# Sixteen-expert diffusion step on one Trainium2 core: earlier third and later expert blocks, expert rows fetched by plain loads, first input weights issued after the fourth modulation block

## The reference, cut to what matters

```
h  = rmsnorm(x) * (1 + scale1) + shift1;  P = h @ w_in          # 12 MB of weights
x  = x + gate1 * concat(A, B, C, D) @ w_out                     # attention, scan, window attention, DFT
h2 = rmsnorm(x) * (1 + scale2) + shift2
x  = x + gate2 * MoE(h2)         # 16 experts, top-1 of 4 groups, then top-2 experts in it
     a = h2 @ w_gate[e]; u = h2 @ w_up[e]; z = silu(a) * u * gates[:, e]; out += z @ w_down[e]
```

## Time and profile before

| | us |
|---|---|
| median of three runs | 1331.93 |
| the profiled execution, its own time | 1326.58 |
| its span, first to last instruction | 1324.6 |
| TensorE busy | 1183.9 |
| VectorE / ScalarE / GpSimd busy | 541.4 / 422.4 / 283.5 |

### The profile page before, as it was taken

One profiled execution on the slowest core, in us unless ns is written; L12 is line 12 of the kernel. 1 busy time (PEld: TensorE's weight loads), 2 busy tenths in 40 slices (PEclk: granted clock), 3 DMA queues, 4 the chain that ended last, 5 costly groups with the idle time before them and its releaser, 6 DMA issues.

```text
span 1324.6 us, 19868 instructions
## 1 busy us (share of the span) xinstructions
PE 1183.9 (89%) x7788; PEld 543.6 (41%) x7788; DVE 541.4 (41%) x1309; ACT 422.4 (32%) x732; POOL 283.5 (21%) x375
## 2 busy tenths in 40 slices
PE   3899899789879999999869989979896999999995
PEld 0555555354423333333234655546343333333332
DVE  1274676733532222221455756585145122211217
ACT  2223444431323333333221334443122433323332
POOL 1230373220021211110510325350102021111022
PEclk9999889789989999999979997997996999999997
DMA  9749531655779999999730313063614999999962
GB/s 365 269 149 161 99 96 69 230 201 223 293 286 390 390 387 382 403 397 377 268 111 2 134 64 97 16 244 134 257 61 166 407 394 385 401 391 379 381 238 92
DMA packets 52722, 324.13 MB, mean 245 GB/s; under 512 B 8457, under 2 KB 8905, under 8 KB 34080
## 3 DMA queue, kind: packets, MB, share of 16 engines
q1 hardware_dynamic: 37568, 286.87, 56.1%
q0 software_dynamic: 13792, 31.42, 9.2%
q10 hardware_dynamic: 1280, 4.72, 0.9%
HBM read 318.70 MB, written 24.31 MB: 259 GB/s over the span
## 4 chain that ended last, share of the span: by engine, by line
PE 68%; DVE 16%; DMA 11%; issue 2%; ACT 2%; another core or an unknown queue 1%; SPq 0%; DVEq 0%; ACTq 0%
PE ps L1917 32%; PE ps L1558 18%; DMA ring<-moe_w_up 7%; PE ps L1806 7%; DVE attT L1155 3%; DVE dbuf L1134 2%; DMA ring<-ada_w 2%; PE ps L1906 2%; PE ps L1569 2%; PE ps L1592 2%; PE ps L1729 1%; PE ps L1700 1%; DVE small L1260 1%; DMA ring<-w_out 1%
## 5 line engine op out<-in xcount | busy, mean ns | idle before, releaser
L1917 PE MATMUL ps<-ring,dbuf 128*32 128x512 f32 x3072 | 433.2, 602 | 18.3 <-ACT dbuf L1003 7.2
L1917 PE MATMUL ps<-extra,dbuf 128*32 128x512 f32 x1536 | 210.7, 595 | 3.6 <-DMA ring<-moe_w_up 3.6
L1917 PEld LDWEIGHTS ps<-ring,dbuf 128*32 128x32 f32 x3072 | 119.3, 111 | 220.6 <-issue 213.4
L1558 PE MATMUL ps<-ring,extra 128*128 128x512 f32 (+1 forms) x384 | 149.4, 549 | 0.0
L1558 PE MATMUL ps<-extra,ring 128*128 128x384 f32 (+1 forms) x384 | 124.1, 470 | 7.6 <-ACT extra L810 5.1
L1917 PEld LDWEIGHTS ps<-extra,dbuf 128*32 128x32 f32 x1536 | 61.2, 110 | 133.3 <-issue 133.1
L744 POOL DMA_INDIRECT expert_rows<-big,lst x28 | 26.5, 946 | 417.6 <-DVE big L1476 417.6
L999 ACT ACTIVATE big<-ps 96x512 f32<-96x512 f32 x32 | 34.5, 1079 | 226.6 <-issue 169.9
L1558 PEld LDWEIGHTS ps<-ring,extra 128*128 128x128 f32 x384 | 73.9, 194 | 69.5 <-issue 66.0
L1454 DVE COPY dbuf<-ps 128x384 f32<-128x384 f32 x32 | 17.8, 558 | 202.6 <-PE ps L1906 199.1
L1558 PEld LDWEIGHTS ps<-extra,ring 128*128 128x128 f32 x384 | 73.9, 202 | 52.9 <-issue 9.4
(11 more groups left out here) (300 smaller groups left out, 1484.2 us busy)
## 6 DMA issues: line engine op xcount, KB each, us to landing
ring<-moe_w_up SPq DMA_DIRECT2D x30, 2048.0 KB
ring<-ada_w SPq DMA_DIRECT2D x24, 2048.0 KB
ring<-moe_w_down SPq DMA_DIRECT2D x18, 2048.0 KB
ring<-moe_w_gate SPq DMA_DIRECT2D x16, 2048.0 KB
extra<-moe_w_gate SPq DMA_DIRECT2D x16, 2048.0 KB, 17.1
extra<-moe_w_down SPq DMA_DIRECT2D x14, 2048.0 KB, 20.0
ring<-w_in SPq DMA_DIRECT2D x12, 2048.0 KB
ring<-w_out SPq DMA_DIRECT2D x4, 2048.0 KB
```

What stands on the lines that cost most here:

```text
L1558: ins = pe.matmul(out, a, b, start=(n == 0), stop=(n == len(pairs) - 1))
L1917: return pe.matmul(p[QT * g:QT * (g + 1), :], a, w, start=start, stop=stop, tile_position=(0, QT * g))
```

## The change

- SP no longer holds block 3. In layer 0 block 4 is held until the first gather has landed, in layer 1 no block is (`HELD`). The look at the overflow number comes after block 5; where there is overflow, blocks 3 to 5 are loaded a second time after it (`blocks_again`).
- The clearing of the table and the six scatters of records are inside POOL's overflow branch.
- The expert rows come back through six plain loads, 512 KB each, issued by SP after a layer's last block and before the next layer's first. All rows are loaded; those of the last two experts are multiplied by zero: `kept` is 0 or 1. ScalarE (ACT) multiplies tile by tile the first choice (three copies of 1024 columns with a scale per row, after the last turn's copy), DVE adds the second choice times its factor, one operation a tile, for tile 2 too.
- `completed` adds both halves of PE's part to y first, then does gate and x with 1024 columns each. POOL does no sums and no clearing of `yr`.
- The first `w_in` block waits until all four `ada` blocks have landed.

```diff
+HELD = [4, None]
...
-                    if l and i_n == 1:
-                        for t in range(NT):
-                            sp.wait_ge(d_yr[t], 32 * l)
+                    if l == 0 and i_n == len(ADA_FIRST):
+                        for b in range(len(ADA_FIRST)):
+                            sp.wait_ge(landed[SLOT_OF[ISSUE[0][b]]], 16)
...
-                        if j == 3:
-                            overflow_weights(l)
+                        if j == HELD[l]:
                             sp.wait_ge(d_g[0], 16 * (NE // 2 * l + 1))
...
+                        expert_block(l, j, landed[n])
+                        if j == ESLOTS - 1:
+                            overflow_weights(l)
...
+                for b in range(2):
+                    sp.wait_ge(d_sc[b], 16 * ((NE - LATE) // 2) * (l + 1))
+                for t in range(NT):
+                    for k in range(2):
+                        sp.dma_start(yr[k][:, t, :], yrow.rearrange("(t p k) d -> t k p d", t=NT, k=2)[t, k]).then_inc(d_yr[t], 16)
...
+                    if last:
+                        act.wait_ge(s_late, l + 1)
+                        for t in range(NT):
+                            act.wait_ge(d_yr[t], 32 * (l + 1))
+                            act.activation(yr[0][:, t, :], yr[0][:, t, :], ACT.Copy, scale=kept[:, t:t + 1]).then_inc(s_kept, 1)
...
-                    step(dve.tensor_tensor(y, y, yr[1][:, t, :], ALU.add))
-                    step(dve.tensor_tensor(y, y, gate[:, min(t, 1), :], ALU.mult))
-                    step(dve.tensor_tensor(x[:, t, :], x[:, t, :], y, ALU.add))
+                    step(dve.scalar_tensor_tensor(out=y, in0=yr[1][:, t, :], scalar=kept[:, NT + t:NT + t + 1], in1=y, op0=ALU.mult, op1=ALU.add))
...
+                        y = yr[0][:, t, b * 512:(b + 1) * 512]
+                        release(dve, dve.tensor_tensor(y, y, p, ALU.add), job)
+                    y = yr[0][:, t, :]
+                    step(dve.tensor_tensor(y, y, gate[:, min(t, 1), :], ALU.mult))
+                    dve.tensor_tensor(x[:, t, :], x[:, t, :], y, ALU.add).then_inc(s_x, 1)
```

More of the change, by code:

```diff
@@ L390, in hybrid_step @@
         d_skew = sem("skew_rows_written")
-        d_tab, d_hrow, d_slot = (sem(n) for n in ("table_cleared", "hidden_rows_stored", "slots_scattered"))
+        d_hrow = sem("hidden_rows_stored")
         s_inpl, s_lst = sem("slot_columns_ready"), sem("slot_lists_ready")
@@ L396, in hybrid_step @@
         s_sel, s_pay, s_ovt, s_nov = (sem(n) for n in ("choices_ready", "slots_ready", "overflow_table_ready", "overflow_count_ready"))
-        s_late, s_sum2, d_init = sem("late_rows_known"), sem("tile_two_summed"), sem("expert_rows_first_written")
+        s_late, s_kept, d_init = sem("late_rows_known"), sem("rows_of_kept_picks"), sem("expert_rows_first_written")
         sync_passed, pool_passed = sem("sync_passed"), sem("pool_passed")
-        ov = [{k: sem(f"ov{l}_{k}") for k in ("weights_landed", "tensor", "vector", "scalar", "list_landed", "gathered", "stored")} for l in range(L)]
+        ov = [{k: sem(f"ov{l}_{k}") for k in ("weights_landed", "tensor", "vector", "scalar", "list_landed", "gathered", "stored",
+                                        "table_cleared", "slots_scattered", "blocks_again")} for l in range(L)]
         table = nc.dram_tensor("slot_table", (NE * T, 4), U32, kind="Internal").ap()
@@ L524, in overflow_weights @@
                     for q in range(3, ESLOTS):
-                        if BEFORE["expert", l, q]:
-                            block_read(sp, BEFORE["expert", l, q])
+                        blk = ("expert", l, q)
+                        sp.wait_ge(landed[SLOT_OF[blk]], 16 * NTH[blk])
                     sp.wait_ge(s_ovt, l + 1)
@@ L535, in overflow_weights, with expert_block @@
                         sp.sem_inc(sync_passed, 1)
+                    for q in range(3, ESLOTS):
+                        expert_block(l, q, o_["blocks_again"])
+            def expert_block(l, j, landed_):
+                kind_, e_ = queued(j)
+                view, kc = {"a": (moe_w_gate, KC), "u": (moe_w_up, KC), "dn1": (moe_w_down, FC)}[kind_]
+                sp.dma_start(slot_of(SLOT_OF["expert", l, j]).rearrange("p (k n) -> p k n", k=kc),
+                             view[l].rearrange("e (p k) n -> e p k n", p=P)[e_]).then_inc(landed_, 16)
             for l in range(L):
-                gview = moe_w_gate[l].rearrange("e (p k) n -> e p k n", p=P)
-                uview = moe_w_up[l].rearrange("e (p k) n -> e p k n", p=P)
-                dview = moe_w_down[l].rearrange("e (p k) n -> e p k n", p=P)
                 for i_n, blk in enumerate(ISSUE[l]):
@@ L570, in _ @@
                                      src.rearrange("(k p) n -> p k n", p=P)).then_inc(landed[n], 16)
+                moved(sp, ("lst", l))
+                sp.wait_ge(s_pay, l + 1)
+                for s in range(2):
+                    for b in range(2):
+                        moved(sp, ("gbc", l, 1, s, b))
+                for b in range(2):
+                    sp.wait_ge(d_sc[b], 16 * ((NE - LATE) // 2) * (l + 1))
+                for t in range(NT):
+                    for k in range(2):
+                        sp.dma_start(yr[k][:, t, :], yrow.rearrange("(t p k) d -> t k p d", t=NT, k=2)[t, k]).then_inc(d_yr[t], 16)
             for t in range(NT):
@@ L703, in _ @@
                 gather(1)
-                pool.wait_ge(s_pay, l + 1)
-                for t in range(NT):
-                    for k in range(2):
-                        pool.indirect_dma_start(table, bass.IndirectOffsetOnAxis(slotu[:, t, k:k + 1], 0), pay[:, t, k, :],
-                                                None).then_inc(d_slot, 16)
                 pool.wait_ge(s_lst, 2 * l + 2)
@@ L713, in _ @@
                 with pool.If(n_ov > 0):
+                    pool.dma_start(table.rearrange("(p r) w -> p (r w)", p=P), slots0[:, 0:4 * NE * NT]).then_inc(o_["table_cleared"], 16)
+                    pool.wait_ge(o_["table_cleared"], 16)
+                    pool.wait_ge(s_pay, l + 1)
+                    for t in range(NT):
+                        for k in range(2):
+                            pool.indirect_dma_start(table, bass.IndirectOffsetOnAxis(slotu[:, t, k:k + 1], 0), pay[:, t, k, :],
+                                                    None).then_inc(o_["slots_scattered"], 16)
+                    pool.wait_ge(o_["slots_scattered"], 16 * 2 * NT)
                     pool.wait_ge(s_ovt, l + 1)
-                    pool.wait_ge(d_slot, 16 * 2 * NT * (l + 1))
                     with pool.Fori(0, n_ov) as r:
@@ L732, in _ @@
                         gather(e + 2)
-                    if e == EXP_PER_BODY:
-                        for s in range(2):
-                            for b in range(2):
-                                moved(pool, ("gbc", l, 1, s, b))
-                        for k in range(2):
-                            step(pool.memset(yr[k], 0.0))
                     if l == 0 and e == 1:
```

40 lines of the change are left out of this document (6 added, 34 removed).

## The result

The changed kernel takes **1312.7 us** (median of four executions, 1309.87 to 1314.31) where the kernel before takes 1329.76 in the same comparison (1322.63 to 1332.45): ratio 0.988, 95% interval 0.983 to 0.992. It is 1.2% faster.

A forecast was written before the change was run, and what follows sets the result against it. The chain was taken as mostly TensorE, with the expert stages' weight stream slightly slower and late near their end. Terms summed to -6.9 us, 1331.93 to 1325.0; half of 3.2 us surplus lead gave 1323.4, range 1316 to 1330.5.

The forecast's parts named there:

- I take the waits as gone: -1.9 and -5.8: Expert stages, layers 0 and 1: earlier blocks 3 to 5 end TensorE's waits for up blocks, -1.9 and -5.8 us.
- counted half of 3.2 us: Sum: lead gained, 10.9 us, exceeds the waits seen, 7.7, by 3.2; half counted for slower executions' longer waits.
- Two blocks and two gathers are 5.0 MB, less than the 5.93 that were moved: Layer 0's expert stage: with block 3 issued early, no backlog is left at 388 us, when block 6 goes out.
- The tails, "-0.3" and "+0.9": End of each layer after the last down product, new DVE order: -0.3 us in layer 0, +0.9 in layer 1.
- They were covered, except that they slowed DVE's: Tails: POOL's three sums, which go, were covered except for slowing DVE's; no size given.
- The start, "+0.4": Start: first input block issued after the last modulation block lands; first input product 0 to 0.9 us later, taken as +0.4.
- my bound of +2: Start: upper bound of the loss, +2 us, if the input block's issue is slower still.
- The head, "-0.2": Head of the expert stages: table clearing and scatters are covered; DVE loses one operation, -0.2 us, layer 1 alone.
- The first: Rival 1, head and tails: the gaps beside POOL's gathers go too, 9.3 us in all, 1314.1 us; chance 0.15.
- The rule that I held against it: Against rival 1: by the instruction-fetch rule the gaps come from the loop that ended before, and stay; time stays 1323.4.
- The second rival: Rival 2, expert stages: the stream stays late, only half of the 7.7 us goes, 1328.9 us; chance 0.20.
- The third: Rival 3, tails: row loads hold up ACT before the last down product, 9 us a layer, 1343 us; chance 0.05.

The follow-up runs named there:

- before_start: The kernel before with only the start's wait added (first input weights wait for the four modulation blocks): 1330.09 us, ratio 1.0027.
- before_dvesum: The kernel before with POOL's three wide additions of tile 2 in the tails done by DVE: 1322.94 us against 1326.47, ratio 0.998.
- nostart: The changed kernel without its start's wait for the four modulation blocks: 1308.25 us (before 1328.33 beside it).
- before_again: The kernel before, unchanged, profiled a second time: 1324.17 us.
- after_again: The changed kernel, unchanged, run once more beside two versions of it: 1312.01 us (before 1327.43).

## Why the prediction was wrong

**The rows of one execution were taken as the kernel's.** That is the root. The profiled execution of before had gaps that ended in "remote" on ACT, DVE and POOL, and they delayed PE by some 16.5 us in all. While PE stood at the head of layer 0, the stream of blocks ran on and won lead, and in the tails POOL's sums got out of DVE's way. So the same rows showed too small a price at two other places: 7.7 us of waiting for blocks, where five executions of before and its variants without gaps have 12.4 to 16.6, and tails 3.1 and 2.5 us too short. The total did not tell them apart, 1326.58 and 1324.17 us, but partly by luck, since the first execution was 7.3 us ahead before its first gap.

**"I take the waits as gone: -1.9 and -5.8", -7.7: too small, this step failed.** The method was right and its two numbers came from the wrong execution: the waits at which I capped the gain, and the backlog of layer 0, which is 7.8 us and not 3.0 where PE does not stand at the head. In the executions without gaps the waits are large enough to use most of the lead of some 15 us: early blocks alone gave -13.2 us, of which 8.3 to 12.5 are seen as less waiting in the stages (12.4 to 16.6 down to 4.1). I had seen the hint (the slower executions "must have lost their 5 us somewhere, and waits of the stream are what can grow") and counted half of 3.2 us for it. That the waits of layer 0 would vanish was also wrong: 2.1 us stayed. "Two blocks and two gathers are 5.0 MB, less than the 5.93 that were moved" used the 17.7 us of the gap; between block 4 (376.78) and block 6 (388.68) there are 11.9 us, in which 343 GB/s are 4.1 MB, so by my arithmetic 0.9 MB or 2.4 us of backlog were left. Block 3 went out at 363.15 and not near 354, since PE must have read its slot first, which I had overlooked; it cost little, as from 372 to 376.78 the link moved only 177 GB/s.

**The tails, "-0.3" and "+0.9": right against the rows, wrong for the kernel.** From the last copy to the last `normalize` it is 21.7 us before and after in layer 0 (652.10 to 673.80 after), and 22.6 and 23.0 in layer 1 (1282.05 to 1305.06). Against executions without gaps the new order gains 3.1 and 2.0, and with SP's loads it gave -5.4. "They were covered, except that they slowed DVE's" was the sentence in which the term was hidden: the slowing is 5.6 us in the tail of layer 0 (2.79 + 3.25 + 3.25 less 3 x 1.23) and 4.5 in layer 1 (1.65 + 3.25 + 3.25), on the path, and I left it without a number.

**The start, "+0.4": wrong.** The first input block is used 13.03 us after its issue, where I had 8.06 and 2 for the small loads. The block of 8.06 us was not alone either: SP issued the next behind it within 2.1 us, and three more by 293.6. What differs is what moved beside the first block: 3.78 MB in 13.03 us at 290 GB/s, 0.93 of them POOL's small loads, against 2.45 MB in 8.06 us at 304 GB/s. Between the two profiled executions the first input product is 3.7 us later; over all of them it begins at 42.7 to 46.2 us without the wait and at 45.8 to 47.7 with it. Measured: +2.7 alone and 3.8 to 4.4 in the changed kernel, beyond my bound of +2. The clock has no part that can be told: the stretch ahead of the first input product had 0.84 with the wait in `before_start` and 0.59 without it in `before_dvesum` (33.5 to 46 us), and the 240 products took 82.8 to 85.8 us without the wait too, 85.77 in `nostart`.

**The head, "-0.2": not settled.** The table's move gave 1.2 alone and 2.6 when undone, and neither is clear of the noise. In layer 1 I had looked only at the gather behind the early blocks. It landed 4.33 us after its issue, but the store of hidden rows ahead of it took 10.82 us. From block 2 to the turns it is 28.8 us instead of 26.6, and most of this is hidden behind DVE's router work: to the first expert product it is 31.0 instead of 30.6.

**The rivals.** The first had the right time, 1314.1, by luck: the gaps did go, but they stood in one of 20 profiled executions, and the kernel before once more and six versions of it had none. What the parts give was measured against medians of 20 to 26 executions, and adds up to the whole without the gaps. "Against: DVE ran its router work without gaps beside POOL's indirect issues" was the better half of it. The rule that I held against it (the Trainium skill, Runtime: NRT & Kernel Launch, section Instruction fetch mechanics: a taken branch outside the window makes the engine fetch code by DMA) would have kept the gaps where they were; the traces do not agree, since the same code ran without them (`before_again`). The second rival (the stream stays late) is refuted by the 4.1 us left. The third (ACT held by the row loads) shows 0.7 and 1.4 us in layer 0 with SP's loads, nothing with a price; with POOL's gathers it is most of 6.5 us (6.0 in the tail of layer 0).

**What the sum would have been** with terms from executions without gaps: waiting -11.7 (14.5 in the mean of five before, 2.8 in the mean of three after), tails -5.1, start +2.7 to +3.8, head 0 to -1.2: -13.0 to -15.3, against 15.4 to 17.1 measured, whose intervals reach down to 10 and 12. What remains is within the noise. Layer 1's mixer is 4.4 us shorter in the profiled execution after (first input product to block 2: 684.20 to 988.39 before, 680.75 to 980.59 after), but `after_again`, the same kernel, has 681.60 to 985.48, so this is a difference between executions and not a term.

## What to carry to other kernels

Where a stream runs beside the engine that the chain shows, the waits for it are what is left after every other delay: a gap at the head of the stage hides part of them, and changes the backlog too. So judge a stream by its own arithmetic (bytes against PE's time, backlog at the first late block), done on more than one execution, and do not cap a gain in lead at the waits of one. And profile the kernel before twice: idle time that ends in an unknown queue on several engines at once may belong to that execution alone.

## What the runs showed of the hardware

- **Gaps that end in "remote".** In the first execution ACT and DVE stood for up to 6.4 us at the head of layer 0's stage and in both tails, POOL for 2.3 us at the head. A queue of instructions was read by DMA near two of the three places. In the stretches of before 368 to 382 and 641 to 646 us its rows are:

```profile
q14 instruction: 2, 0.02, 0.4%
...
q14 instruction: 1, 0.01, 1.5%
```

  In the third place no instruction queue has a row from 1283 to 1293 us, although gaps of 4.4 and 3.3 us end there. The second execution read instructions at like points of the program (one row each of 645 to 650 and 375 to 383 us) without a gap. So it is not shown that the gaps are waits for instructions; what made them in that execution is open. None of the other 19 profiled executions has one.
- **DVE beside POOL.** A wide addition or multiplication of two operands in SBUF, 1.23 us alone, took up to 3.25 us while POOL did the same kind of work (its own 2.3 to 3.4 us each).
- **A block of 2.1 MB beside small loads.** At the start the first of several blocks was used 13.0 us after issue, with 0.93 MB of POOL's small loads moving beside it; the first `w_out` block, also with others behind it but only one small transfer of 96 KB beside it, took 8.0 to 8.1 us.
- **A store beside a full stream.** The last of layer 1's three stores of hidden rows (512 KB) landed 10.8 us after its issue, with four blocks issued 12 us before it, and the first gather waited for it. The median of the six such stores went from 4.0 to 10.3 us; with the early blocks alone (`before_early`) it is 10.3 too.

```profile
993.38 10.82 DMA hidden_rows<-big
1005.06 4.33 DMA dbuf<-hidden_rows,lst
```
